# Scan's reloads in 256 KB pieces that SyncE issues one at a time

## The reference

```
def rwkv7_scan(inputs, s0):
    def step(s, inp):
        r_t, w_t, k_t, v_t, kk_t, a_t = inp
        sa = jnp.einsum('bhvk,bhk->bhv', s, -kk_t)
        s = (s * w_t[:, :, None, :] + sa[..., None] * (kk_t * a_t)[:, :, None, :]
             + v_t[..., None] * k_t[:, :, None, :])
        return s, jnp.einsum('bhvk,bhk->bhv', s, r_t)
...
def rglru_direction(xb, lp, d, h0):
    xc = causal_dwconv(xb.astype(jnp.float32), lp['conv_w'][d], lp['conv_b'][d])
    rg = jax.nn.sigmoid(block_diag_linear(xc, lp['wa'][d], lp['ba'][d]))
    ig = jax.nn.sigmoid(block_diag_linear(xc, lp['wx'][d], lp['bx'][d]))
    log_a = -LRU_C * rg * jax.nn.softplus(-lp['lam'][d])
    a = jnp.exp(log_a)
    bt = jnp.sqrt(-jnp.expm1(2.0 * log_a)) * (ig * xc)
    _, h = lax.associative_scan(lru_combine, (a, bt), axis=1)
...
m_lat = (silu_c @ w_mod[layer] + b_mod[layer])[:, None, :]
```

## Time and profile before

| | us |
|---|---|
| Median of 3 runs | 4354.61 |
| The profiled execution's own time | 4352.81 |
| Its span on the core | 4351.0 |
| Mean granted TensorE clock over the span | 0.928 of 2.4 GHz |
| Scan, of which bodies 1 to 16 | 1118 to 2450, of which 1190.9 to 2340.9 |

### The profile page before, as it was taken

One profiled execution on the slowest core, in us unless ns is written; L12 is line 12 of the kernel. 1 busy time (PEld: TensorE's weight loads), 2 busy tenths in 40 slices (PEclk: granted clock), 3 DMA queues, 4 the chain that ended last, 5 costly groups with the idle time before them and its releaser, 6 DMA issues. The chain is left out here.

```text
span 4351.0 us, 118962 instructions
## 1 busy us (share of the span) xinstructions
PE 3732.7 (86%) x50925; PEld 3292.5 (76%) x50925; DVE 2396.6 (55%) x4390; ACT 1828.6 (42%) x2997; POOL 1242.1 (29%) x1250
## 2 busy tenths in 40 slices
PE   4799999999688888888888589795499999999992
PEld 2678888888577777777777488673399999999992
DVE  3246766610256666666666655334766666666664
ACT  3246666521144444444445443231144444444444
POOL 2223333311345555555453155000001010101010
PEclk7899999999899999999899799897699999999996
DMA  5235555522432333332331475341267676767675
GB/s 172 69 125 180 181 172 176 172 95 73 116 76 73 91 81 83 86 86 78 86 81 43 145 224 171 115 153 50 93 196 213 207 213 194 214 197 222 196 213 198
DMA packets 566347, 610.27 MB, mean 140 GB/s; under 512 B 65938, under 2 KB 471252, under 8 KB 564820
## 3 DMA queue, kind: packets, MB, share of 16 engines
q1 hardware_dynamic: 515540, 487.01, 36.4%
q0 software_dynamic: 21536, 76.56, 6.1%
q10 hardware_dynamic: 28768, 39.16, 2.8%
HBM read 443.09 MB, written 159.40 MB: 138 GB/s over the span
## 5 line engine op out<-in xcount | busy, mean ns | idle before, releaser
L339 DVE TENSOR_TENSOR moe_w_lo<-moe_w_lo_whole,moe_w_hi 128x2048 fp32r<-128x2048 f32 (+1 forms) x258 | 453.5, 1758 | 263.2 <-ACT moe_w_hi L517 187.8
L460 PE MATMUL moe_h<-moe_xt_hi,moe_w_hi 128*128 128x256 f32 x2048 | 582.1, 284 | 16.3 <-DVE moe_xt_lo L339 15.0
L460 PE MATMUL moe_h<-moe_xt_lo,moe_w_hi 128*128 128x256 f32 x2048 | 580.2, 283 | 0.0
L460 PE MATMUL moe_h<-moe_xt_hi,moe_w_lo 128*128 128x256 f32 x2048 | 580.1, 283 | 0.0
L1792 PE MATMUL inward_pp<-u_u_hi,inward_w_hi 128*128 128x512 f32 (+1 forms) x1360 | 527.6, 388 | 20.8 <-POOL inward_w_lo L1952 20.8
L1792 PE MATMUL inward_pp<-u_u_lo,inward_w_hi 128*128 128x512 f32 (+1 forms) x1360 | 516.1, 379 | 0.0
L1792 PE MATMUL inward_pp<-u_u_hi,inward_w_lo 128*128 128x512 f32 (+1 forms) x1360 | 515.8, 379 | 0.0
L460 PEld LDWEIGHTS moe_h<-moe_xt_hi,moe_w_hi 128*128 128x128 f32 x2048 | 393.2, 192 | 28.7 <-issue 25.0
L460 PEld LDWEIGHTS moe_h<-moe_xt_lo,moe_w_hi 128*128 128x128 f32 x2048 | 393.4, 192 | 3.8
L460 PEld LDWEIGHTS moe_h<-moe_xt_hi,moe_w_lo 128*128 128x128 f32 x2048 | 393.3, 192 | 0.0
L412 POOL DMA_INDIRECT scratch_x<-moe_ys,moe_who x32 | 70.6, 2205 | 911.0 <-DVE moe_ys L568 906.1
(11 more groups left out here) (376 smaller groups left out, 9924.8 us busy)
## 6 DMA issues: line engine op xcount, KB each, us to landing
moe_w_lo_whole<-in_moe_w SPq DMA_DIRECT2D x387, 512.0 KB, 5.1
scratch_ops<-inward_ops SPq DMA_DIRECT2D x72, 514.0 KB, 3.8
scan_over<-scratch_ops SPq DMA_DIRECT2D x72, 512.0 KB, 9.9
inward_w_lo_whole<-in_w_in SPq DMA_DIRECT2D x38, 512.0 KB, 4.5
scan_aq<-scratch_ops SPq DMA_DIRECT2D x36, 516.0 KB, 5.0
scratch_gates<-inward_out SPq DMA_DIRECT2D x64, 256.0 KB, 2.1
all_late<-in_w_mod POOLq DMA_DIRECT2D x32, 512.0 KB, 5.1
rest_modsum<-scratch_gates SPq DMA_DIRECT2D x64, 256.0 KB, 3.9
```

What stands on the lines that cost most here:

```text
L339: return nc.vector.tensor_tensor(x_lo, x, x_hi.bitcast(F32), ALU.subtract)
L460: mm = nc.tensor.matmul(hb[ft % 2][m][:, 0:CAP], w_, x, start=(k == 0 and part == 0), stop=(k == KD - 1 and part == 2))
```

## The change

- SP's reloads are cut into pieces of about 256 KB: `aq` into one DMA for each direction d (258 KB), `over` into one for each direction and half (256 KB); `ob` stays (256 KB). A reload is 10 DMAs now, an own reload 4.
- Behind each of these (but for those before the loop) SP waits until it has landed before it issues the next.
- `store` waits, behind each unit's 4 DMAs, until they have landed. The wait for the stores at the stage's end goes.
- The loop's order is now reload(it+1), store(it), reload_own(it).
- PE's and ACT's waits count the pieces.
- POOL's part of the modulation matrix is loaded in two halves of 256 KB with a semaphore each, the next part's half issued as soon as this part's is used up.
- ACT's row of latents comes in four DMAs of 256 KB: all four at the start, else two at the last window of a row and two at the next.

```
--- before.py
+++ after.py
@@ -2171,7 +2171,7 @@
         s_root, s_wbd, s_cols, s_ctx, s_lat, s_z = (n.sem(f"lru_{x}") for x in ("sqrt", "weights", "columns", "context", "latents", "stored"))
         s_y = [n.sem(f"y_stored{u}") for u in U]
         s_masks, s_sum, s_zero = n.sem("masks_loaded"), n.sem("mod_summed"), n.sem("state_zero")
-        s_wm = n.sem("wm_loaded")
+        s_wm = [n.sem(f"wm_loaded{x}") for x in range(2)]
         block = ctx.enter_context(nc.Block())
 
         def flat(x):
@@ -2211,26 +2211,39 @@
 
         @block.sync
         def _(sp):
-            def load(it, own, rest):
+            def load_own(it, wait):
                 src = env["ops"][:, it]
                 for u in U:
-                    if own:
-                        sp.dma_start(aq[u][:, it % 2, :, :], src[u][:, :, 2 * G:4 * G + 4]).then_inc(s_aq[u][it % 2], 16)
-                    if rest:
-                        sp.dma_start(ob[u][:, :, :], src[u][:, :, 4 * G + 4:OPS]).then_inc(s_ob[u], 16)
-                        sp.dma_start(over[u][0:HD, :, :], src[u][HD:P, :, 0:4 * G]).then_inc(s_over0[u], 16)
-                        sp.dma_start(over[u][HD:P, :, :], src[u][0:HD, :, 0:4 * G]).then_inc(s_over1[u], 16)
+                    for d in range(2):
+                        sp.dma_start(aq[u][:, it % 2, d, :], src[u][:, d, 2 * G:4 * G + 4]).then_inc(s_aq[u][it % 2], 16)
+                        if wait:
+                            sp.wait_ge(s_aq[u][it % 2], 32 * (it // 2) + 16 * d + 16)
+
+            def load(it, wait):
+                src = env["ops"][:, it]
+                for u in U:
+                    sp.dma_start(ob[u][:, :, :], src[u][:, :, 4 * G + 4:OPS]).then_inc(s_ob[u], 16)
+                    if wait:
+                        sp.wait_ge(s_ob[u], 16 * it + 16)
+                for d in range(2):
+                    for u in U:
+                        sp.dma_start(over[u][0:HD, d, :], src[u][HD:P, d, 0:4 * G]).then_inc(s_over0[u], 16)
+                        if wait:
+                            sp.wait_ge(s_over0[u], 32 * it + 16 * d + 16)
+                        sp.dma_start(over[u][HD:P, d, :], src[u][0:HD, d, 0:4 * G]).then_inc(s_over1[u], 16)
+                        if wait:
+                            sp.wait_ge(s_over1[u], 32 * it + 16 * d + 16)
 
             def reload(it):
                 for u in U:
                     PE[u].wait(sp, "tK", it)
-                load(it + 1, False, True)
+                load(it + 1, True)
 
             def reload_own(it):
                 for u in U:
                     PEc[u].wait(sp, "Y3", it)
                     DVc[u].wait(sp, "Sb3", it)
-                load(it + 2, True, False)
+                load_own(it + 2, True)
 
             def store(it):
                 for u in U:
@@ -2239,19 +2252,20 @@
                         for h in range(2):
                             dst = env["y"][d, bass.ds(it, 1), :, u * P + h * HD:u * P + (h + 1) * HD].rearrange("o (c s) v -> s (o c) v", s=HD)
                             sp.dma_start(dst, y[u][64 * h:64 * h + 64, 4 * d:4 * d + 4, :]).then_inc(s_y[u], 16)
+                    sp.wait_ge(s_y[u], 64 * (it + 2))
 
             n_main = sum(k for _, k in CONST_SIZES)
-            load(0, True, True)
+            load_own(0, False)
+            load(0, False)
             sp.dma_start(masks[:, :], t["consts"][:, n_main:n_main + len(MASKS) * P]).then_inc(s_masks, 16)
-            load(1, True, False)
+            load_own(1, False)
             reload(0)
             for it in range(LAST + 1):
                 if it + 2 <= LAST:
                     reload(it + 1)
+                store(it)
+                if it + 2 <= LAST:
                     reload_own(it)
-                store(it)
-            for u in U:
-                sp.wait_ge(s_y[u], 64 * (LAST + 2))
 
         @block.tensor
         def _(pe):
@@ -2289,7 +2303,7 @@
                 oA, oB = of_ops(aq[u], b, 0), of_ops(ob[u], None, 0)
                 xV, xK = (of_ops(over[u], None, k * G) for k in range(2))
                 if r == 0:
-                    pe.wait_ge(s_aq[u][b], half * 16 + 16)
+                    pe.wait_ge(s_aq[u][b], half * 32 + 32)
                     pe.wait_ge(s_ob[u], 16 * it + 16)
                     DV[u].wait(pe, "W5", it - 1)
                     two(u, ("L", 2, oA, oB), ("Lt", 3, oA, oB))
@@ -2298,8 +2312,8 @@
                     DV[u].wait(pe, "T0", it)
                     both_of("B", u, oB, aq[u][:, b], 0, False)
                 elif r == 2:
-                    pe.wait_ge(s_over0[u], 16 * it + 16)
-                    pe.wait_ge(s_over1[u], 16 * it + 16)
+                    pe.wait_ge(s_over0[u], 32 * it + 32)
+                    pe.wait_ge(s_over1[u], 32 * it + 32)
                     DV[u].wait(pe, "Lb1", it)
                     both_of("K", u, xK, over[u], 2 * G, True)
                 elif r == 3:
@@ -2443,7 +2457,8 @@
                 if part == "context":
                     act.dma_start(raw[:, 0:CTX], src[:, 1:1 + CTX]).then_inc(s_ctx, 16)
                 else:
-                    act.dma_start(raw[:, CTX:], src[:, LAT0:LAT0 + SEQ]).then_inc(s_lat, 16)
+                    n_ = SEQ // 4
+                    act.dma_start(raw[:, CTX + part * n_:CTX + (part + 1) * n_], src[:, LAT0 + part * n_:LAT0 + (part + 1) * n_]).then_inc(s_lat, 16)
 
             def load_weights(g):
                 j, d = g // 2, g % 2
@@ -2458,7 +2473,7 @@
                 if m == 0:
                     act.wait_ge(s_ctx, 16 * (j + 1))
                 else:
-                    act.wait_ge(s_lat, 16 * (j + 1))
+                    act.wait_ge(s_lat, 64 * (j + 1))
                 if k:
                     DVt.wait(act, "t3", k - 1)
                 lat = raw[:, CTX:].rearrange("p (r w) -> p w r", w=GRID_W)
@@ -2484,7 +2499,11 @@
                 if k % (2 * NG) == NG and j + 1 < NJ:
                     load_raw(j + 1, "context")
                 elif k % (2 * NG) == 2 * NG - 1 and j + 1 < NJ:
-                    load_raw(j + 1, "latents")
+                    for part_ in range(2):
+                        load_raw(j + 1, part_)
+                elif k % (2 * NG) == 0 and k:
+                    for part_ in range(2, 4):
+                        load_raw(j, part_)
 
             def gates(k):
                 j, d, m, i = lru_of(k)
@@ -2565,7 +2584,8 @@
             for s in (ACw, ACg, ACq):
                 s.start(act)
             load_raw(0, "context")
-            load_raw(0, "latents")
+            for part_ in range(4):
+                load_raw(0, part_)
             act.wait_ge(s_zero, 4)
             load_weights(0)
             through(act, body)
@@ -2729,16 +2749,17 @@
             silu = env["silu"]
             units = stack.unsqueeze(1).broadcast_to([P, 8, HD])
 
-            def load(part_):
+            def load(part_, x):
                 if part_ < 4 * KD:
-                    at, half = part_ // 2, part_ % 2
-                    pool.dma_start(wm, w_mod[:, NJ * half:NJ * (half + 1), 2 * D + at * G:2 * D + (at + 1) * G]).then_inc(s_wm, 16)
+                    at, k = part_ // 2, NJ * (part_ % 2) + NJ // 2 * x
+                    pool.dma_start(wm[:, NJ // 2 * x:NJ // 2 * (x + 1), :], w_mod[:, k:k + NJ // 2, 2 * D + at * G:2 * D + (at + 1) * G]).then_inc(s_wm[x], 16)
 
             def add(part_, count):
                 at, half = part_ // 2, part_ % 2
                 dst = env["modsum"][:, at * G:(at + 1) * G]
-                pool.wait_ge(s_wm, 16 * (part_ + 1))
                 for k in range(NJ):
+                    if k % (NJ // 2) == 0:
+                        pool.wait_ge(s_wm[k // (NJ // 2)], 16 * (part_ + 1))
                     to = part if half or k else dst
                     pool.tensor_scalar(to, wm[:, k, :], silu[:, NJ * half + k, 0:1], None, ALU.mult).then_inc(s_sum, 1)
                     count += 1
@@ -2747,7 +2768,8 @@
                         pool.tensor_tensor(dst, dst, part, ALU.add).then_inc(s_sum, 1)
                         count += 1
                         pool.wait_ge(s_sum, count)
-                load(part_ + 1)
+                    if k % (NJ // 2) == NJ // 2 - 1:
+                        load(part_ + 1, k // (NJ // 2))
                 return count
 
             def start_solve(it):
@@ -2779,7 +2801,8 @@
                 PO[u].start(pool)
             POl.start(pool)
             pool.wait_ge(s_masks, 16)
-            load(0)
+            for x in range(2):
+                load(0, x)
             count = 0
             for it in range(LAST + 2):
                 more, first = it <= LAST, 4 * (it - 1)
```

19 lines of the change are left out of this document (11 added, 8 removed).

## The result

The changed kernel takes 4481.29 us (median of 4 runs, 4476.9 to 4497.76) against 4355.99 for the one before (4 runs, 4348.41 to 4364.31): a ratio of 1.0294, 95% interval 1.0262 to 1.0326. That is 125 us slower. The forecast was 4465, 112 us slower, in a range of 4380 to 4600.

What follows compares the result with a forecast made beforehand. PE, busiest, was taken to stall while its code waits behind reload data; SP's waits then make a chain of 33.5 + 8.6 + 13.4 + 24.0 = 79.5 us against 72.2, +117 - 5 = +112: 4465 us, range 4380 to 4600.

Steps and rivals of the forecast that it cites:

- last landing to tK: From aq's last landing to the next reload's issue (tK): 19.9 + 2.0 to evacuation + 2.1 low clock, 24.0 us.
- body 0: The first loop body has its aq early and only loses its stall: -5 us.
- T: Time from one 256 KB piece's issue to the next's, landing plus hand-over: 3.3 + 0.05, 3.35 us for all pieces.
- Leg A: From the reload's issue (tK) to Y3: 41.5 us before, then 33.5 by ten pieces, PE's own way 31.4.
- The most that the change can win: PE's stalls with no visible cause, 121.6 us over 16 bodies, taken away: about 120 us.
- The cold clock: PE idles some 15 us ahead of round 0, then runs 4.9 us at clock 0.50: 2.1 us a body.
- POOL and ACT: nothing: POOL's matrix halves and ACT's row in four parts are covered by other waits: 0, POOL within -5 to +26 us.
- Fast pieces: Rival: lone pieces land nearer 2.1 than 3.3 us; +33, 4386 us, or no change at 2.15 a piece; chance 0.12.
- slow pieces: Rival: each piece goes through other traffic and lands in 3.9 us; +246, 4599 us; chance 0.13.
- no effect: Rival: the waits do nothing, pieces land before SP would issue the next anyway; 4353 us; chance 0.02.
- The faster rival: Stalls and PE's low clock go, pieces under 2.98 us; at 2.15 a piece -66, 4287 us; chance 0.07.
- The Trainium skill's figure: A DMA takes about 2.0 us plus bytes at 436 GB/s: 256 KB in 2.6 us, sum +33.

Runs made afterwards that it cites:

- e1: The changed kernel with the own reload of aq moved ahead of the 8 stores, every wait kept: 4356.1 us, 1.0009 of the kernel before.
- e6: The changed kernel without the waits behind the stores, which stay ahead of aq: 4431.1 us, 1.0189 of the kernel before.
- e2: The changed kernel with the own reload ahead of the stores and only the reload of ob and over waited for: 4254.7 us, 0.9774 of the kernel before.
- e7: The kernel before with ob and over loaded once for group 0 and never again, aq always group 0's: 4233.4 us, one run.
- e3: The kernel before with only the halves of POOL's matrix and the four parts of ACT's row: 4353.6 us, ratio 1.0007.
- e9: The kernel before with a wait behind each DMA of the reload, nothing cut: 4276.0 us, ratio 0.9831.
- e4: The changed kernel's pieces with none of SP's waits, own reload ahead of the stores: 4307.4 us, 0.9892 of the kernel before.
- e8: The changed kernel, own reload first, only the reload waited for, over's pieces issued two at a time: 4254.4 us, 0.9775 of the kernel before.

## Why the prediction was right

The forecast's chain is what the chip ran: reload, stores, own reload, round 0. Moving the stores out of it (e1) and taking their waits away (e6) changes a body by about what the chain says. That the sum came within 0.4 us of a body is in part luck: four terms were off and cancel. The terms, with means over the bodies of the changed kernel:

| | forecast | measured |
|---|---|---|
| reload, 10 pieces | 33.5 | 36.8 |
| 8 stores with their waits | 8.6 | 9.5 |
| own reload, 4 pieces | 13.4 | 11.0 |
| last landing to tK | 24.0 | 22.6 |
| body | 79.5 | 79.9 |
| bodies, 16 times (72.2 before in the forecast, 72.0 measured) | +117 | +126 |
| body 0 | -5 | -5 (reload of body 1 at 1212.8 before, 1207.6 now) |

- **T.** One value for all pieces was wrong both ways: `ob` has 3.2, `over` 3.7 and `aq` 2.7. The text saw that `over` reaches half the partitions, and left it at 3.3. Pieces under 3 us apart were named as a sign of being wrong, and those of `aq` are 2.75 apart. The errors, 3.3 up and 2.4 down, nearly cancel, which is luck.
- **Leg A.** PE's own way to Y3 was put at 31.4 with no stall left. It is 32.5 with 3.2 us of stalls in it, so 29.3 without: the stalls did not go (52.1 us are left at the largest row, where 121.6 stood), and a gain by the clock that the forecast left out was there (e2). It made no difference, since SP's 36.8 ended the leg.
- **The most that the change can win** was put at 120 us, all of it stalls. Without a reload 117 us are won (e7), but of the 7.7 us by which leg A is shorter there the stalls are 5.2; the rest goes with the clock, which is never low in leg A there.
- **The cold clock, 2.1 us.** The clock was low for 4.6 us behind the last landing, near the 4.9 of the forecast: all of the 2.1 us from landing to evacuation, and 2.5 behind it (0.9 to 7.1). It seems to have cost something: over 15 bodies the way from evacuation to tK grows from 19.3 us by 0.49 for each us at the low clock (correlation 0.94), 1.2 us in the mean. It does not show in the sum, since this way is 20.5 us in the mean as it was before (20.4). A reason may be that unit 0 is 5.5 us ahead of unit 1 now instead of 1.5, so that its part is done within the wait; no run tests this.
- **Body 0.** The -5 is right in size, not in cause. The first reload comes 1.7 us earlier, and body 0 is 3.5 us shorter, of which 2.2 are stalls; 5.3 us of stalls are left in it.
- **POOL and ACT: nothing,** shown by e3. The cover named for POOL was its wait for ACT; the time went into a wait for DVE.
- **Order and waits.** The text priced the stores' place by their duration, 8.6; e1 gives 7.5 of 9.5, since `aq` ahead of them goes slower, 12.5 instead of 11.0.
- **The rivals.** Fast pieces, slow pieces and no effect are out by the landings, 3.4 us in the mean over the 14 pieces. The faster rival needed the stalls gone, the clock back and pieces under 2.98 us at the mean; only the clock came, in leg A (29.3 there, 29.3 measured).
- **The Trainium skill's figure** ("DMA: Bandwidth & Descriptors", "Anatomy of one DMA"), an estimate of 2.6 us for 256 KB by its fit for the software path, is near what `aq` measured (2.7) and far from `over` (3.7). By it the sum was +33; the measured change is +125.

## What to carry to other kernels

A DMA queue whose issuer waits for each landing turns its bytes into a chain of landings: count every wait between an event and the transfer that the next stage needs first, and put that transfer first. Pacing pays where nobody waits for the data: the reload takes 36.5 us and has the 46 from tK to the next round 0. Where the next step waits for it, issue at once: without the waits for `aq` and the stores behind it a body is 6.0 us shorter (e1 against e2). When a change mixes both, take it apart: here the paced reload alone was 2.3% faster, and with the order and the waits around it 2.9% slower. And a stall costs more than its own length where PE's clock falls in it, so look at the clock of the work behind it too.

## What the runs showed of the hardware

- PE's code comes by DMA, and a burst of data holds it up. In the kernel before 96 of 96 stalls end 1.2 to 1.8 us behind a 16 KB packet of the queue of instructions (counted under e7). They are up to 7.8 us long with 2.5 MB in flight, at most 2.8 without that reload (e7), 2.6 where it goes 256 KB at a time (e2), 3.1 at 512 KB at a time (e9).
- In such stalls PE's clock falls, and it is low behind them too (0.50 for 4.9 us): 8.1 us of each leg A at 0.50 before, 0.6 with the reload paced. PE's busy time in leg A is 2.2 us shorter then (e2).
- The same bytes in twice the DMAs, all issued at once, stall PE less (5.8 instead of 7.1 us a body, 1.1% of the time; e4). The cause is open.
- 256 KB from DRAM land in 2.7 us over 128 partitions in rows of 2 KB and in 3.7 over 64 partitions in rows of 4 KB. Rows, partitions and the other traffic differ together here, and no run parts them. Issued in pairs, these halves land in 3.9 at the median (3.3 to 5.1, e8).
